# Two output tiles of the second feed-forward computed from x without the norm's root and shift

## What is computed

```python
x = x + g1 * (mixed @ w_out[l])

h = rms_norm_2(x, norm2_g[l]) * (1 + sc2) + sh2
u = causal_depthwise_conv(h @ w_up[l], conv_w[l], conv_b[l])
u_gate, u_val = jnp.split(u, 2, axis=-1)
x = x + g2 * ((jax.nn.silu(u_gate) * u_val) @ w_down[l])
```

## Time and profile before

| | |
|---|---|
| median of 3 executions | 1436.36 us |
| the profiled execution | 1436.72 us, its span 1434.8 us |
| mean granted TensorE clock | 0.987 |
| TensorE matmul busy | 1383.8 us, 96% of the span |
| VectorE busy | 887.0 us, 62% |
| ScalarE busy | 590.0 us, 41% |
| DMA, mean | 102 GB/s |
| chain that ended last | TensorE 91%, VectorE 5%, ScalarE 2% |

### The profile page before, as it was taken

How to read it: one execution, slowest core, us unless ns; L and a number is a source line. 1 busy time by engine, 2 the same in 40 slices (tenths; PEclk the granted TensorE clock), 3 DMA queues, 4 the chain that set the end, 5 groups by cost and what they waited for, 6 DMA issues and landing times.

```text
span 1434.8 us, 18347 instructions
## 1 busy us (share of the span) xinstructions
PE 1383.8 (96%) x6316; PEld 1094.8 (76%) x6316; DVE 887.0 (62%) x1454; ACT 590.0 (41%) x967; POOL 70.4 (5%) x128
## 2 busy tenths in 40 slices
PE   7999999999989999999997999799989999999999
PEld 5777777767768888888884787567668888888887
DVE  5666677777587777774337677566556656655222
ACT  5445445543353233233225524466445444444221
POOL 4000000000001111120000000000000000000000
PEclk9999999999999999999998999899999999999999
DMA  5322212213315555664441112011122232233332
GB/s 188 99 74 74 74 60 74 75 57 103 114 49 175 198 192 190 192 200 153 125 133 65 60 60 74 31 63 55 60 70 88 88 102 91 99 102 105 102 95 84
DMA packets 42321, 146.74 MB, mean 102 GB/s; under 512 B 5392, under 2 KB 5664, under 8 KB 42272
## 3 DMA queue, kind: packets, MB, share of 16 engines
q1 hardware_dynamic: 34448, 120.39, 25.7%
q0 software_dynamic: 7824, 25.70, 5.4%
HBM read 143.97 MB, written 2.10 MB: 102 GB/s over the span
## 4 chain that ended last, share of the span: by engine, by line
PE 91%; DVE 5%; ACT 2%; issue 1%; DMA 0%; DVEq 0%; ACTq 0%
PE bank L601 64%; PE bank L716 12%; PE bank L673 3%; PE bank L738 2%; PE bank L641 2%; PE bank L757 2%; PE bank L941 1%; PE bank L775 1%; PE bank L628 1%; ACT w_hi L1105 1%; DVE w_lo L1585 1%; DVE hbuf L1634 0%; DVE gate_last L1775 0%; DVE gate_a L1775 0%; PE bank L778 0%
## 5 line engine op out<-in xcount | busy, mean ns | idle before, releaser
L1585 DVE TENSOR_TENSOR w_lo<-raw,w_hi 128x1024 fp32r<-128x1024 f32 (+2 forms) x225 | 271.6, 1210 | 165.2 <-ACT w_hi L1105 160.4
L1105 ACT ACTIVATE w_hi<-raw 128x1024 fp32r<-128x1024 f32 (+2 forms) x225 | 233.1, 1037 | 301.4 <-PE bank L601 278.1
L601 PE MATMUL bank<-h_hi,w_hi 128*128 128x512 f32 x872 | 346.2, 397 | 0.0
L601 PE MATMUL bank<-h_lo,w_hi 128*128 128x512 f32 x872 | 340.4, 390 | 0.0
L601 PE MATMUL bank<-h_hi,w_lo 128*128 128x512 f32 x872 | 340.2, 390 | 0.0
L601 PEld LDWEIGHTS bank<-h_hi,w_hi 128*128 128x128 f32 x872 | 164.2, 188 | 41.6 <-issue 8.0
L601 PEld LDWEIGHTS bank<-h_hi,w_lo 128*128 128x128 f32 x872 | 164.1, 188 | 34.9
L601 PEld LDWEIGHTS bank<-h_lo,w_hi 128*128 128x128 f32 x872 | 164.2, 188 | 33.8 <-issue 1.2
L601 PE MATMUL bank<-f_hi,w_lo 128*128 128x512 f32 x352 | 136.9, 389 | 0.0
L601 PE MATMUL bank<-f_hi,w_hi 128*128 128x512 f32 x352 | 136.9, 389 | 0.0
L601 PE MATMUL bank<-f_lo,w_hi 128*128 128x512 f32 x352 | 136.9, 389 | 0.0
(11 more groups left out here) (305 smaller groups left out, 1860.0 us busy)
## 6 DMA issues: line engine op xcount, KB each, us to landing
raw<-in_w_up SPq DMA_DIRECT2D x66, 512.0 KB, 3.3
raw<-in_w_mix SPq DMA_DIRECT2D x48, 512.0 KB, 3.3
ada<-in_w_ada POOLq DMA_DIRECT2D x96, 256.0 KB, 3.3
raw<-in_w_down SPq DMA_DIRECT2D x32, 512.0 KB, 3.5
raw<-in_w_in SPq DMA_DIRECT2D x25, 512.0 KB, 3.3
raw<-in_w_gate SPq DMA_DIRECT2D x22, 512.0 KB, 3.3
raw<-in_w_out SPq DMA_DIRECT2D x16, 512.0 KB, 3.3
raw<-in_w_down SPq DMA_DIRECT2D x16, 384.0 KB, 3.4
```

The lines of the kernel that those rows point to most:

```text
L601: last = pe.matmul(to[:, :], wt[:, slot, k, :], act_[:, rhs0 + k, :], start=(k == first and n == 0), stop=(k == K - 1 and n == 2))
L1105: act.activation(w_hi[:, s, k0:K, :], raw[:, s, k0:K, :], ACT.Copy).then_inc(hi_ready[s], 1)
L1585: dve.tensor_tensor(w_lo[:, s, k0:K, :], raw[:, s, k0:K, :], w_hi[:, s, k0:K, :].bitcast(F32), ALU.subtract).then_inc(split_ready[s], 1)
```

## The change: what it does

- **Unscaled input.** During w_out_2, behind each tile's square, ScalarE computes `u_hi = a_k * x_k` rounded and VectorE its rest `u_lo`: 8 more instructions on each.
- **Shift products.** After w_out_2 and ahead of `sum_squares`, TensorE multiplies the two raw weight tiles (float32, slots 2 and 0) with the column of shifts: 16 products with one moving column each, into two columns of bank S1. VectorE copies those to `shifts`.
- **Two units on u.** After `sum_squares` TensorE computes T1 and T0 from `u`, one whole unit after the other, in place of `two_units` on `h`; then `up()`, which now waits for `h_ready` at each `k`.
- **Afterwards.** When `h` is done, VectorE multiplies T1 and T0 in place by `rstd`, ScalarE adds `shifts` to each in place, and the convolution goes on as before.
- **Order.** The split of slot 1 now stands ahead of the root on ScalarE and ahead of the norm on VectorE. SyncE waits for the shift products before it overwrites slot 2 and slot 0.

```diff
@@ sync, ffn_rounds
                 load(0, tile(gate, 0))
                 load(1, tile(up, up0 + 1))
+                if up0:
+                    sp.wait_ge(shift_done, 2)
                 down_unit(down, 0, 2)
@@ tensor
+            def shift_products():
+
+                for n, slot in enumerate((2, 0)):
+                    pe.wait_ge(split_ready[slot], w.next(split_ready[slot]))
+                    for k in range(KD):
+                        last = pe.matmul(S1[:, n:n + 1], raw[:, slot, k, :], modc[:, 24 + k:25 + k], start=(k == 0),
+                                         stop=(k == KD - 1))
+                    last.then_inc(shift_done, 1)
+
+            def unscaled_units():
+
+                pe.wait_ge(u_ready, w.next(u_ready, times=KD - 1))
+                unit(T1, 2, u_hi, u_lo, ready=u_ready, late=u_ready)
+                unit(T0, 0, u_hi, u_lo, ready=u_ready)
...
-                two_units((T0, T1), (0, 2))
                 if not squares:
-                    up()
+                    unscaled_units()
+                    up(h_ready)
                 else:
+                    two_units((T0, T1), (0, 2))
                     unit(S1, 1, h_hi, h_lo)
...
+            shift_products()
             sum_squares()
             ffn(conv_gd, conv_vd, False)
@@ scalar
+            def unscaled_hi(k):
+
+                act.activation(u_hi[:, k, :], xT[:, k, :], ACT.Identity, scale=mod_a[:, 1, k:k + 1]).then_inc(u_hi_r, 1)
+
             for t in range(KD - 1):
                 split_hi(t % SLOTS, by_halves=(t == 0))
                 x_tile(t % 2, t)
+                unscaled_hi(t)
             x_tile(1, 7)
+            unscaled_hi(7)
             w.start(unit_done, "ffn_2")
+            split_hi(1)
             inverse_rms()
-            split_hi(1)
             modulated_hi(lambda k: mod_a[:, 1, k:k + 1], lambda k: modc[:, 24 + k:25 + k])
...
+            act.wait_ge(shift_read, 1)
+            for n, bank_ in enumerate((T1, T0)):
+                act.wait_ge(u_scaled, n + 1)
+                then(act.activation(bank_[:, :], bank_[:, :], ACT.Identity, bias=shifts[:, n:n + 1]))
             conv_round(0, T0, T1, 2, conv_first)
@@ vector
+            def unscaled_lo(k):
+
+                dve.wait_ge(u_hi_r, w.next(u_hi_r))
+                dve.scalar_tensor_tensor(out=u_lo[:, k, :], in0=xT[:, k, :], scalar=mod_a[:, 1, k:k + 1],
+                                         in1=u_hi[:, k, :].bitcast(F32), op0=ALU.mult, op1=ALU.subtract).then_inc(u_ready, 1)
...
                     add_squares(t % 2)
+                unscaled_lo(t)
+            split_lo(1)
+            dve.wait_ge(shift_done, 2)
+            dve.tensor_copy(shifts[:, :], S1[:, 0:2]).then_inc(shift_read, 1)
             modulated_lo()
-            split_lo(1)
+            w.start(unit_done, "ffn_2")
+            for slot, bank_ in ((2, T1), (0, T0)):
+                dve.wait_ge(unit_done[slot], w.next(unit_done[slot]))
+                dve.tensor_tensor(bank_[:, :], bank_[:, :], rstd[:, :], ALU.mult).then_inc(u_scaled, 1)
```

More of the change, by code:

```diff
@@ L218, in build @@
         modc = sb("modc", [48])
+        shifts = sb("shifts", [2])
         mod_a = sb("mod_a", [2, 8])
@@ L283, in build @@
         assert gla_end <= nc.sbuf_usable_end, gla_end - nc.sbuf_usable_end
+        (u_hi, u_lo), u_end = region(work_at + 24576, ("u_hi", [KD, S], F32R), ("u_lo", [KD, S], F32R))
+        assert u_end <= big_at + 2 * NF * S * 4
         (qk_sq,), qk_end = region(gla_end, ("qk_sq", [2, S], F32))
@@ L391, in build @@
         stored = signal("stored", 16)
+        u_hi_r, u_ready, u_scaled = signal("u_hi_r"), signal("u_ready"), signal("u_scaled")
+        shift_done, shift_read = signal("shift_done"), signal("shift_read")
         def col(name, k=0):
@@ L856, in two_tiles, with up @@
                     pair()
+            def shift_products():
[9 more added lines that the diff above has]
+                unit(T0, 0, u_hi, u_lo, ready=u_ready)
             def ffn(read0, read1, squares):
-                def up():
+                def up(fresh=None):
                     pe.wait_ge(read1, w.next(read1, ahead=1))
-                    unit(G1, 1, h_hi, h_lo)
+                    unit(G1, 1, h_hi, h_lo, fresh=fresh)
                 def gate():
```

## The result

The changed kernel takes **1440.58 us** (median of 6 executions, 1439.75 to 1441.77). The kernel before, counted again beside it, takes 1434.97 us (6 executions, 1434.37 to 1436.68). The ratio is 1.0035, with a 95% interval of 1.0024 to 1.0045: slower, by more than the 0.2% that can be told. The forecast was 1440.4 in 1437.2 to 1442.8.

What follows compares the result with a forecast made beforehand. TensorE, busy 96% of the span, was taken as the bound, with the start of gate() the number to follow. 0.55 (gate()) + 2.2 + 1.3 (clock) = 4.05, added to the median 1436.4, gave 1440.4 us; range 1437.2 to 1442.8.

Steps and rivals of the forecast that it cites:

- The likeliest case: Whole kernel: the later gate() and both clock losses make it slower, 1440.4 us; chance 0.40.
- u_hi and u_lo, hidden: In w_out_2: at most 0.88 us for each instruction, hidden in both engines' waits, so 0.
- Products, 0.111 each, 3.55 us: Between w_out_2 and the sum of squares: 32 instructions at 0.111 take 3.55 us, bounds 1.3 and 7.1.
- Rival 2: Shift products: weight loads don't set the step, products take under 1.5 us, not slower, 1436.4 us; chance 0.15.
- The clock behind the products, +1.3 (0 to 1.7): In the sum of squares: near-empty array lowers TensorE's clock, delaying the norm by 1.3 us (0 to 1.7).
- Scaling, shifts, taps, first tap +0.8 in all: Behind the norm: multiplies and shift additions let the first convolution step start at 1084.15 instead of 1083.35, 0.8 later.
- The stall of 5.7 one unit later: Ahead of gate(): TensorE's wait of 4.66 is not removed but sits one unit later, at 5.7 us.
- the 5 to 6 that the prediction asked for as a sign: Ahead of a unit of L608: idle time of 5 to 6 us shows the forecast right, under 3 wrong.
- The clock behind the stall, 2.2 (1.4 to 3.1): From gate() on: the clock falls behind the 5.7 us wait and costs 2.2 us (1.4 to 3.1) in full.
- SyncE's wait, 0: SyncE's loads behind the products: gate tile 1 arrives near 1070, needed at 1085, so 0.
- The sum: Whole kernel: 0.55 for gate(), 2.2 and 1.3 for the clock, +4.05 us in all.
- one split, slot 0's: Ahead of gate(): this split ends at 1089.1 instead of 1088.28, so gate() starts 0.55 us later.

Runs made afterwards that it cites:

- e1: Changed kernel without the one-column shift products, SyncE's wait for them and the copy of their result (shifts set to zero): 1436.72 us, 1.001 of before.
- e12: The changed kernel run again with no edit: 1440.77 us, 1.0035 of the kernel before.
- e8: Changed kernel without scaling T1 and T0 by the root and without adding the shifts, all waits kept: 1437.45 us, 1.0016 of before.
- e3: Changed kernel with the 16 one-column products replaced by 16 matmuls of 512 columns: 1438.04 us, 1.0017 of the kernel before.
- e2: Changed kernel with the products behind the sum of squares and VectorE's copy of the shifts behind the norm: 1434.90 us, 0.9996 of before.
- e10: Changed kernel with one product ahead of each three matmuls of the units on u, and both slots split early: 1437.02 us, 1.0012 of before.
- e5: Changed kernel with slot 0 split between the two scalings, ahead of the convolution: 1440.27 us, 1.0032 of the kernel before.
- e6: Changed kernel with slot 0 split between the scalings and slot 1's second split at the first round's end: 1439.03 us, 1.0031 of before.
- e4: Kernel before plus only the one-column products and SyncE's wait for them, result unused: 1439.82 us, 1.003 of the kernel before.
- e9: Changed kernel with one product ahead of each three matmuls of the two units on u: 1433.99 us, 0.9991 of the kernel before.
- e11: Changed kernel with all products in the first unit on u, two ahead of each three matmuls, and both slots split early: 1436.16 us, 1.0003 of before.
- e7: Changed kernel with the products behind the sum of squares and both slots split early: 1434.79 us, 0.9993 of the kernel before.

## Why the prediction was right

The likeliest case came: 1440.58 against 1440.4. Its steps:

- **u_hi and u_lo, hidden**: yes. w_out_2 takes 54.82 us from its first matmul to t0 before and 54.81 in the changed kernel, the first products start where it ends, and in e1 the first matmul on u follows the squares without a wait.
- **Products, 0.111 each, 3.55 us**: 3.57 in e12 and 3.84 in the profiled execution, where the clock had fallen already in their last part. The row of L969 was the right one to lean on. Rival 2 did not come. The Trainium skill (TensorE: Matmul & The Clock Gate, Back-to-back issue gap) gives about 25 ns as the issue floor for so few columns, but says in the same section that in a stream where each matmul has its own weight load both set the step. The prediction quoted only the floor; 0.112 us apart is 4.5 times that.
- **The clock behind the products, +1.3 (0 to 1.7)**: it fell in every trace in which the products stand together, and in the profiled execution it cost 1.8 us in the squares and 0.3 in the products themselves. **This term was mis-sized**: 2.1 there, above its upper bound, and 1.6 in e12, near it. I had bounded it by the four instructions of the squares alone and had not let the clock fall while the products still ran. Root, first tap and `gate()` are 4.73, 2.81 and 2.63 behind before, against 3.97, 2.1 and 1.85 by the sum, so 0.7 to 0.8 later than forecast (0.2 to 0.3 in e12).
- **Scaling, shifts, taps, first tap +0.8 in all**: the path was right. From the loaded table to the first tap it was forecast at 1.65 and takes 1.52; e8 prices it at 1.4. The first tap moved less than the norm did (2.81 against 4.73), as the norm first used up the 3.39 that this tap waited for its bank before.
- **The stall of 5.7 one unit later**: 4.38 and 5.54, the first below the 5 to 6 that the prediction asked for as a sign. TensorE was later than I had put it, as the first unit on u ran at half clock too; that half clock is free, since it only shortens the stall.
- **The clock behind the stall, 2.2 (1.4 to 3.1)**: 1.6 and 2.5 in the two profiled executions of the changed kernel, 1.4 in e3 and 2.8 in e1.
- **SyncE's wait, 0**: right for this order (e2), and not a rule: in e10 it costs 2.2.
- **The sum**: 4.05 against 3.5 by the spans of the two profiled executions and 5.6 by the medians. At equal t0 the second `up()` is 4.3 behind before, and 4.6 in e12, and what follows it takes the same 340.7 us in all three. The rest of the 5.6 lies ahead of w_out_2, where t0 varies, or outside the span, and was not located further. **That 1440.58 came within 0.2 of 1440.4 is partly luck**: the slowdown was 1.6 larger than forecast, and the median of before, now from six executions, came out 1.4 below the 1436.36 of three to which the forecast was added. The profiled execution of before lies 1.75 above the new median.

What the prediction did not see is how many things stand behind the norm: it followed one split, slot 0's, to the stall, and e5 and e6 show that without it the wait is hardly shorter in sum: 1.40 + 2.98 and 1.14 + 3.11, against 4.38.

## What to carry to other kernels

Work that fills a stall of the bound engine gains only as much as the chain behind the stall lets later work start; here that chain let the second `up()` start at 30.4 in the three best orders, and the gain there was 1.9 us, not the 4.66 of the stall. So before filling a stall, follow the waited-for chain to the next thing that needs it, and put nothing ahead of the step that feeds it: the same 32 instructions cost about 4 us ahead of the sum of squares (e1, e4) and nothing behind it (e2). In a row they brought the clock down, one ahead of each three full matmuls they did not (e9).

## What the runs showed of the hardware

**A TensorE that is busy all the time in the record can lose its clock.** 32 one-column instructions in a row keep TensorE 100% busy in the record, and the clock fell behind or within them in the eight traces that have them so (the changed kernel twice, e2, e4 to e8). It held with full columns in the same place (e3), with one product ahead of each three full matmuls (e9, e10), and with two (e11).

**The same wait does not always bring the clock down.** The trace of before has a wait of 2.71 us at 347.16, in code that no experiment touches. e7 has it at the same time, with 2.69. A stretch behind it, in e7 (before's is the first of the earlier trace rows, at 0.52):

```profile
348.30:351.80 3.50, 3.50 (x17) 2.87 (x16) 3.27 (x6) 1.10 (x2) 0.00 (x0) 1.00 0.00 0
```

17 matmuls instead of 11. Over the fourteen traces the clock fell there in eight (before, changed, e1, e2, e4, e9, e10, e12) and held in six, which is a good part of why w_out_2 ends anywhere between 1059.6 and 1062.1: on the mean at 1061.62 in the eight and at 1060.23 in the six. Of the waits in the second feed-forward, 2.12 brought it down (e11), and 2.94 (e8), 2.98 (e5), 3.08 (e10) and 3.11 (e6) did not. Each fall behind a wait cost 1.4 to 3.0 us where it was priced, as much as most of the edits here. The Trainium skill (the same page, What's actually happening) says that the number of slow matmuls varies from run to run of one kernel; the seven executions of e5 fall into two groups, 1437.6 to 1438.3 and 1440.3 to 1441.8, with mean clocks of 0.989 to 0.990 and 0.986 to 0.987. That this is the clock behind its wait of 2.98 is likely and was not seen, as only one of them was traced.

What stays open is whether e9 beats before: its interval reaches 1.0001.
